# A first weight quarter with a transfer of its own, products by halves of two quarters, and the norm behind them

## The chip, the cores and the metric

One core of one Trainium2 chip. The metric is the device time of one execution in microseconds; the median of three runs stands for a kernel. TensorE is called PE in the rows, VectorE DVE, ScalarE ACT, GpSimd POOL and SyncE SP.

## The reference, cut to what matters

Two transformer blocks run one after the other on 256 tokens of width 1024. Only the first steps of the first block are touched:

```python
h = rmsnorm(x, attn_norm[i])            # x times 1/sqrt(mean(x*x)+eps), times a gain per column
proj = h @ w_in[i]
mq, mk, mv, rq, rk, rv, rg = jnp.split(proj, split_points, axis=-1)
moba_out = ...                          # attention with ALiBi: scores minus slope times distance
ret = ...                               # retention: (q k^T) * decay, times v
ret_out = head_groupnorm(ret, ret_norm[i]) * jax.nn.silu(rg)
```

Everything is float32 in the reference. The kernel forms each float32 product from three products of a high part and a low part.

## The kernel before, in words

**Weights.** All weights lie in HBM as a stream of quarters, 128 partitions x 1024 columns (512 KB) each, in the order of use. SP loads two quarters ("a half" of the stream's blocks) per transfer into `raw`, which has a ring of six quarters; after the first three transfers each next one waits until GpSimd is through with two quarters (semaphore `lo_done`). For each quarter ScalarE writes the rounded high part `w_hi` (`hi`, L635), GpSimd the low part `w_lo = raw - w_hi` in two instructions of 512 columns (`lo`, L594), and TensorE then takes the quarter (`await_quarter`) for 24 products of 256 columns or 12 of 512 columns, three per pair of 128x128 tiles (`three`, L1164). ScalarE keeps four quarters ahead (LEAD), and from the seventh on it waits for `quarter_done` of the quarter six before.

**Blocks of the stream.** Four quarters are a block. The first are RQ (quarters 0 to 3), RK (4 to 7), RV (8 to 11), MQ (12 to 15). A block's result goes to a pair of PSUM banks; pairs 0 and 1 are used in turn, so RV, the third, waits until VectorE has stored RQ out of the first pair (`await_pair`, semaphore `pair_free0`), and MQ until RK is stored (`pair_free1`).

**Order at the start.** Each engine's order is written out by hand. SP: the two halves of x, then three weight transfers. ScalarE: the squares of the second half of x (L657) and their root (L662), the high parts `h_hi` of the turned x (`norm_hi`, L670) with the first two `hi` between them, `hi` of quarters 2 and 3, then `load_constants` (L617 to L620), which issues eight transfers from ScalarE's queue, then `hi` of quarter 4. VectorE: the squares of the first half of x (L2116), the reciprocal root (L2107 to L2110), `widen_root` (L2134), the low parts `h_lo` (`norm_lo`, L2147), the row of roots (L2140); then it waits for all constants, makes the eight ALiBi tables `bias` (L2220), and only then stores RQ and RK (`store_scaled`, L2155) and splits two small inputs (L2227, L2228, L2231). TensorE: 11 filler products on ones (`keep_warm`, L1360), the transposes of x (L1262), 4 fillers, the root spread over a bank (`spread_root`, L1272), 6 fillers, RQ, RK, RV; then MQ with the retention beside it: `ret_scores` (L1343) in front of MQ's first quarter, `ret_out` (L1353) behind it. `ret_out` waits for VectorE's `ret_decay` (L2203) and for the store of RV (L2162), both of which stand behind the tables on VectorE.

```python
act_e.wait_ge(sem("x_loaded"), 16 * NT)
second_squares()
act_e.wait_ge(sem("first_constants"), 32)
norm_hi(0, "attn_norm", (0, 1))
hi(0)
norm_hi(0, "attn_norm", range(2, 6))
hi(1)
norm_hi(0, "attn_norm", (6, 7))
for q in range(2, LEAD):
    hi(q)
load_constants()
```

## Time and profile before

| what | us |
|---|---|
| median of 3 runs (lowest, highest) | 842.63 (842.61, 843.84) |
| the profiled execution's own time | 846.45 |
| its span | 844.6 |
| PE busy in the span | 823.0 |
| POOL busy in the span | 476.0 |

The profile is of one execution; its instructions are told by when they start (us from the span's start) and how long they last. "[2.36 <-DVE work L2155]" behind one is how long its engine sat idle before it and what ended that. The products are pipelined, so their starts are told one after another and their shown lengths overlap.

### The profile page before, as it was taken

To read this page: it belongs to the slowest core of one execution; us is meant where nothing else is said; L and a number is where in the kernel's file an instruction comes from. 1 tells how busy PE (TensorE), PEld (TensorE's weight loads), DVE (VectorE), ACT (ScalarE), POOL (GpSimd) and SP (SyncE) were. 2 spreads that over 40 slices of the span, in tenths; PEclk is the share of its full clock that TensorE was granted. 3 is DMA by queue.
4 is the path that set the end of the run, shared out by engine and by line. 5 is a ranking of instruction groups with operands and counts; after the bars stand their busy time and mean duration, and the time that the engine had idled before them with its cause. 6 is when DMAs were issued, how large, how long until landed. Compare 5 with 4: busy or idle time off the path is not lost.

```text
span 844.6 us, 16277 instructions
## 1 busy us (share of the span) xinstructions
PE 823.0 (97%) x6271; PEld 737.5 (87%) x6271; DVE 496.5 (59%) x1000; ACT 466.3 (55%) x735; POOL 476.0 (56%) x372
## 2 busy tenths in 40 slices
PE   9899999999999999899999999999999999999995
PEld 7899889999999997689988999999889888888883
DVE  3832444682422315663497835347478699999983
ACT  5423654735644466764448433235456578878763
POOL 5997476989999898686854443366868000000000
PEclk9999999999999999999999999999999999999998
DMA  8654144545655554444642213232545689999931
GB/s 315 226 200 177 74 150 175 175 176 199 204 193 199 199 199 150 150 151 150 218 151 100 101 52 102 101 103 100 197 150 177 273 335 370 352 392 340 393 108 50
DMA packets 24141, 160.98 MB, mean 191 GB/s; under 512 B 3200, under 2 KB 3728, under 8 KB 5392
## 3 DMA queue, kind: packets, MB, share of 16 engines
q1 hardware_dynamic: 21456, 154.67, 50.1%
q10 hardware_dynamic: 2624, 5.44, 1.9%
q8 instruction: 44, 0.72, 0.3%
q14 instruction: 17, 0.14, 0.0%
HBM read 157.62 MB, written 1.05 MB: 188 GB/s over the span
## 4 chain that ended last, share of the span: by engine, by line
PE 86%; DVE 7%; ACT 3%; DMA 2%; issue 1%; ACTq 0%; SPq 0%; DVEq 0%
PE bank L1164 72%; PE bank L1713 3%; PE bank L1930 1%; DVE work L2220 1%; DMA row<-dt_bias_dram 1%; PE bank L2047 1%; DMA raw<-weights_dram 1%; DVE work L2529 1%; ACT w_hi L635 1%; PE bank L1262 1%; DVE bank L2589 1%; PE bank L1325 1%; PE bank L1311 1%; DVE best L2588 0%; PE bank L1742 0%
## 5 line engine op out<-in xcount | busy, mean ns | idle before, releaser
L594 POOL TENSOR_TENSOR w_lo<-raw,w_hi 128x512 fp32r<-128x512 f32 x368 | 475.8, 1328 | 175.2 <-ACT w_hi L635 175.1
L1164 PE MATMUL bank<-h_hi,w_hi 128*128 128x256 f32 x864 | 247.4, 286 | 0.5 <-POOL w_lo L594 0.5
L1164 PE MATMUL bank<-h_lo,w_hi 128*128 128x256 f32 x864 | 241.6, 280 | 0.0
L1164 PE MATMUL bank<-h_hi,w_lo 128*128 128x256 f32 x864 | 241.5, 280 | 0.0
L635 ACT ACTIVATE w_hi<-raw 128x1024 fp32r<-128x1024 f32 x184 | 187.9, 1058 | 82.4 <-PE bank L1164 51.2
L1164 PEld LDWEIGHTS bank<-h_hi,w_hi 128*128 128x128 f32 x864 | 162.6, 188 | 4.9 <-POOL w_lo L594 1.4
L1164 PEld LDWEIGHTS bank<-h_hi,w_lo 128*128 128x128 f32 x864 | 163.9, 190 | 0.0
L1164 PEld LDWEIGHTS bank<-h_lo,w_hi 128*128 128x128 f32 x864 | 162.7, 188 | 0.3
L1164 PE MATMUL bank<-w_hi,g_hi 128*128 128x512 f32 x208 | 81.6, 392 | 0.0
L1164 PE MATMUL bank<-w_hi,g_lo 128*128 128x512 f32 x208 | 81.0, 390 | 0.0
L1164 PE MATMUL bank<-w_lo,g_hi 128*128 128x512 f32 x208 | 81.0, 389 | 0.0
L3007 DVE TENSOR_TENSOR w_lo<-raw,w_hi 128x1024 fp32r<-128x1024 f32 x54 | 63.0, 1218 | 5.8 <-ACT w_hi L644 5.6
L1164 PE MATMUL bank<-w_hi,slot_hi 128*128 128x512 f32 x144 | 57.7, 401 | 0.0
L644 ACT ACTIVATE w_hi<-raw 128x1024 fp32r<-128x1024 f32 x54 | 53.6, 1058 | 7.0 <-PE bank L1164 7.0
L1164 PE MATMUL bank<-w_hi,h_hi 128*128 128x512 f32 x128 | 52.6, 411 | 4.0 <-DVE work L2155 2.4
L1164 PE MATMUL bank<-w_hi,slot_lo 128*128 128x512 f32 x144 | 56.3, 391 | 0.0
L1164 PE MATMUL bank<-w_lo,slot_hi 128*128 128x512 f32 x144 | 56.2, 390 | 0.0
L1164 PE MATMUL bank<-w_hi,h_lo 128*128 128x512 f32 x128 | 51.5, 402 | 0.0
L1164 PE MATMUL bank<-w_lo,h_hi 128*128 128x512 f32 x128 | 51.3, 401 | 0.0
L2334 DVE TENSOR_TENSOR bank<-bank,work 128x512 f32<-128x512 f32 x11 | 7.7, 697 | 67.4 <-PE bank L1164 67.4
L1164 PEld LDWEIGHTS bank<-w_hi,g_lo 128*128 128x128 f32 x208 | 39.0, 188 | 8.2
L1164 PEld LDWEIGHTS bank<-w_hi,g_hi 128*128 128x128 f32 x208 | 39.1, 188 | 8.1 <-issue 0.4
(408 smaller groups left out, 1353.9 us busy)
## 6 DMA issues: line engine op xcount, KB each, us to landing
raw<-weights_dram SPq DMA_DIRECT2D x119, 1024.0 KB, 4.8
spare<-weights_dram SPq DMA_DIRECT2D x18, 1024.0 KB, 6.1
tok<-weights_dram SPq DMA_DIRECT2D x9, 1024.0 KB, 5.7
x_sb<-x_dram SPq DMA_DIRECT2D x2, 512.0 KB, 4.6
work<-final_norm_dram ACTq DMA_DIRECT2D x2, 512.0 KB, 5.4
work<-work ACTq DMA_DIRECT2D x8, 128.0 KB, 4.8
work<-constants_dram ACTq DMA_DIRECT2D x1, 640.0 KB, 5.1
con<-constants_dram ACTq DMA_DIRECT2D x1, 520.0 KB, 3.8
```

The lines of the kernel that those rows point to most:

```text
L594: ins = nc.gpsimd.tensor_tensor(w_lo[:, part], raw[:, part], w_hi[:, part].bitcast(F32), ALU.subtract)
L635: nc.scalar.activation(w_hi[:, ring(q)], raw[:, ring(q)], ACT.Copy).then_inc(sem("hi_done"), 1)
L644: nc.scalar.activation(w_hi[:, ring(n)], slot_quarter(i), ACT.Copy).then_inc(sem("slot_hi_done"), 1)
L1164: ins = mm(dst, a, b, start=start and n == 0, stop=stop and n == 2, skip_group_check=True)
L1262: ins = nc.tensor.transpose(bank[turned_bank(n, k)][:, k % 2 * S + t * P:k % 2 * S + (t + 1) * P], x3[:, t, k * P:(k + 1) * P], ident)
L1311: ins = mm(bank[4 + odd][:, t * P:t * P + (t + 1) * P], q3[own, f, t * P:(t + 1) * P], k3[own, kf(f), 0:(t + 1) * P], start=True, stop=True)
L1325: ins = nc.tensor.transpose(bank[6 + n % 2][:, i * P:(i + 1) * P], p[:, i * P:(i + 1) * P], ident)
L1713: ins = mm(bank[b][rows, column + m * w:column + (m + 1) * w], lhs[rows, m, :], rhs[rows, m, :], start=True, stop=True)
L1930: ins = mm(dst, x[t][:, k * P:(k + 1) * P], one_hot[:, t, of], start=t == 0 and x is tok_hi, stop=t == 1 and x is tok_lo, skip_group_check ...
L2047: ins = mm(total[t, c][:, :], one_hot_t[:, tile, t * P:(t + 1) * P], y[:, tile, c * 512:(c + 1) * 512], start=tile == 0 and y is y_hi, sto ...
L2220: V.tensor_scalar(bias[:, h, :], dist, -(HD ** 0.5) * 2.0 ** (-8.0 * (h + 1) / HEADS), None, ALU.mult).then_inc(sem("bias_ready"), 1)
L3007: V.tensor_tensor(w_lo[:, ring(n)], slot_quarter(i), w_hi[:, ring(n)].bitcast(F32), ALU.subtract)\
```

## The change

SP loads quarters 0 and 1 as two transfers, the first with a semaphore of its own. ScalarE makes the high parts of quarters 0 and 1 in halves of 512 columns, between the pairs of `norm_hi`, and does the squares of x and their root only behind `hi(3)`, right ahead of `load_constants`. GpSimd makes the low parts in the order first half of 0, first half of 1, second half of 0, second half of 1. TensorE takes the first halves of quarters 0 and 1, then their second halves, and quarters 2 and 3 by halves too; it spreads the root in front of quarter 3 (into bank 4), and four fillers are gone. VectorE makes `h_lo` first, then the norm, stores RQ before it waits for the constants, then does the splits, stores RK, and makes the tables last. The other edits (`other_sums` in place of `bn_aggr`, and counts raised by seven) change only names and numbers of semaphores.

```diff
@@ -545,7 +545,10 @@
                 sp.dma_start(raw[:, 2 * slot * QUARTER:(2 * slot + 2) * QUARTER], src)\
                     .then_inc(sem(f"half_loaded{slot}"), 16)
 
-            for half in range(3):
+            for part, name in enumerate(("first_loaded", "half_loaded0")):
+                own = slice(part * QUARTER, (part + 1) * QUARTER)
+                sp.dma_start(raw[:, own], weights[0, :, own]).then_inc(sem(name), 16)
+            for half in range(1, 3):
                 load_half(half, half)
             with sp.Fori(0, N_HALVES // 3 - 1) as i:
                 for slot in range(3):
@@ -586,17 +589,21 @@
 
         @block.gpsimd
         def _(pool):
+            def lo_half(r, i):
+
+                part = slice(r % RING * QUARTER + i * (QUARTER // 2), r % RING * QUARTER + (i + 1) * (QUARTER // 2))
+                return nc.gpsimd.tensor_tensor(w_lo[:, part], raw[:, part], w_hi[:, part].bitcast(F32), ALU.subtract)
+
             def lo(n, r):
 
-                pool.wait_ge(sem("hi_done"), n + 1)
-                for i in range(2):
-                    part = slice(r % RING * QUARTER + i * (QUARTER // 2), r % RING * QUARTER + (i + 1) * (QUARTER // 2))
-                    ins = nc.gpsimd.tensor_tensor(w_lo[:, part], raw[:, part], w_hi[:, part].bitcast(F32), ALU.subtract)
-                    if isinstance(n, int) and n == 0 and i == 0:
-                        ins.then_inc(sem("first_low_half"), 1)
-                ins.then_inc(sem("lo_done"), 1)
-
-            for r in range(RING):
+                pool.wait_ge(sem("hi_done"), n + 3)
+                lo_half(r, 0)
+                lo_half(r, 1).then_inc(sem("lo_done"), 1)
+
+            for r, i in ((0, 0), (1, 0), (0, 1), (1, 1), (2, 0), (2, 1), (3, 0), (3, 1)):
+                pool.wait_ge(sem("hi_done"), 2 * r + i + 1 if r < 2 else r + 3)
+                lo_half(r, i).then_inc(sem("lo_done" if i else "first_low_half"), 1)
+            for r in range(4, RING):
                 lo(r, r)
             with pool.Fori(1, N_QUARTERS // RING) as i:
                 for r in range(RING):
@@ -634,6 +641,12 @@
                     act_e.wait_ge(sem("quarter_done"), n - (RING - 1))
                 nc.scalar.activation(w_hi[:, ring(q)], raw[:, ring(q)], ACT.Copy).then_inc(sem("hi_done"), 1)
 
+            def hi_half(q, i):
+
+                act_e.wait_ge(sem("half_loaded0" if q else "first_loaded"), 16)
+                part = slice(q * QUARTER + i * (QUARTER // 2), q * QUARTER + (i + 1) * (QUARTER // 2))
+                nc.scalar.activation(w_hi[:, part], raw[:, part], ACT.Copy).then_inc(sem("hi_done"), 1)
+
             def slot_hi_quarter(i):
 
                 if i >= len(SLOT_ORDER) or SLOT_ORDER[i][1] == WHOLE:
@@ -705,22 +718,25 @@
                     .then_inc(sem("mix_hi_done"), 1)
 
             prepare_root()
-            act_e.wait_ge(sem("x_loaded"), 16 * NT)
-            second_squares()
             act_e.wait_ge(sem("first_constants"), 32)
             norm_hi(0, "attn_norm", (0, 1))
-            hi(0)
-            norm_hi(0, "attn_norm", range(2, 6))
-            hi(1)
+            hi_half(0, 0)
+            hi_half(0, 1)
+            norm_hi(0, "attn_norm", (2, 3))
+            hi_half(1, 0)
+            norm_hi(0, "attn_norm", (4, 5))
+            hi_half(1, 1)
             norm_hi(0, "attn_norm", (6, 7))
             for q in range(2, LEAD):
                 hi(q)
+            act_e.wait_ge(sem("x_loaded"), 16 * NT)
+            second_squares()
             load_constants()
             for q in range(4 * B_WOUT):
                 tick = q - 4 * B_MQ
                 slot = tick - FIRST_TICK
                 if tick == 4:
-                    act_e.wait_ge(sem("other_sums"), 1)
+                    act_e.wait_ge(sem("other_sums"), 8)
                     nc.scalar.activation(stat[:, 128:136], agg[:, :, 1], ACT.Sqrt, bias=eps[:, 1:2])\
                         .then_inc(sem("other_roots"), 1)
                 for n in (2 * slot, 2 * slot + 1):
@@ -1000,7 +1016,7 @@
                 if tick == 4 * (B_PROJ - B_IQ) + 2:
 
                     prepare_root()
-                    act_e.wait_ge(sem("other_sums"), 2)
+                    act_e.wait_ge(sem("other_sums"), 9)
                     nc.scalar.activation(stat[:, 96:112], bank[6][:, 0:16], ACT.Sqrt).then_inc(sem("other_roots"), 1)
                 if tick == 4 * (B_PROJ - B_IQ) + 3:
                     for k in range(4):
@@ -1183,13 +1199,14 @@
             def feature_quarter(n, q, dst, h=(h_hi, h_lo), norm=None, middle=None):
 
 
-                if isinstance(n, int) and n == 0:
-                    pe.wait_ge(sem("first_low_half"), 1)
+                by_halves = isinstance(n, int) and n in (2, 3)
+                if by_halves:
+                    pe.wait_ge(sem("first_low_half"), n + 1)
                 else:
                     await_quarter(n)
                 w = [x.rearrange("p (k c) -> p k c", c=P) for x in quarter(q)]
                 for k in range(KD):
-                    if isinstance(n, int) and n == 0 and k == KD // 2:
+                    if by_halves and k == KD // 2:
                         await_quarter(n)
                     if middle and k == KD // 2:
                         middle()
@@ -1365,10 +1382,25 @@
             pe.wait_ge(sem("x_loaded"), 16 * NT)
             turn_half(0, 0)
             turn_half(0, 1)
-            keep_warm(3, 4, warm)
-            spread_root(0, 2)
             keep_warm(3, 6, warm)
-            feature_project(B_RQ, 0, norm=0)
+
+            def first_quarters_by_halves():
+
+                for half in range(2):
+                    for f in range(2):
+                        if half:
+                            await_quarter(f)
+                        else:
+                            pe.wait_ge(sem("first_low_half"), f + 1)
+                        ins = half_quarter(f, f, bank[0][:, f * S:(f + 1) * S], range(4 * half, 4 * half + 4), 0, f == 0)
+                        if half:
+                            ins.then_inc(sem("quarter_done"), 1)
+
+            first_quarters_by_halves()
+            for f in range(2):
+                if f:
+                    spread_root(0, 4)
+                feature_quarter(2 + f, 2 + f, bank[1][:, f * S:(f + 1) * S])
             pe.wait_ge(sem("root_row_ready"), 1)
             feature_project(B_RK, 1)
             token_project(B_RV, 2)
@@ -2207,20 +2239,15 @@
             V.memset(warm.bitcast(F32), 1.0).then_inc(sem("warm_ready"), 1)
             V.memset(eps[:, 0:1], RMS_EPS)
             V.memset(eps[:, 1:2], GN_EPS).then_inc(sem("constants_made"), 1)
-            dve.wait_ge(sem("x_loaded"), 16 * NT)
-            norm()
-            widen_root()
-            V.tensor_scalar(stat[:, 24:26], stat[:, 4:6], 0.5, None, ALU.mult).then_inc(sem("roots_halved"), 1)
             dve.wait_ge(sem("first_constants"), 32)
             norm_lo(0, "attn_norm")
-            store_root_row(0, 2)
+            dve.wait_ge(sem("x_loaded"), 16 * NT)
+            norm(scratch=bank[5][:, 0:2])
+            widen_root()
+            store_root_row(0, 4)
+            V.tensor_scalar(stat[:, 24:26], stat[:, 4:6], 0.5, None, ALU.mult).then_inc(sem("roots_halved"), 1)
+            store_scaled(B_RQ, 0, rq)
             dve.wait_ge(sem("constants_loaded"), 16 * N_CONSTANT_LOADS)
-
-            for h in range(HEADS):
-                V.tensor_scalar(bias[:, h, :], dist, -(HD ** 0.5) * 2.0 ** (-8.0 * (h + 1) / HEADS), None,
-                                ALU.mult).then_inc(sem("bias_ready"), 1)
-            store_scaled(B_RQ, 0, rq)
-            store_scaled(B_RK, 1, rk)
 
             for hi_, lo_, src in ((p_hi, p_lo, p_raw.rearrange("p (k s) -> p k s", s=S)),
                                   (sm_hi[:, :], sm_lo[:, :], small_raw[:, :])):
@@ -2230,6 +2257,11 @@
 
             V.tensor_scalar(gate_bias[:, :], v("b_gate", 0, 2 * KD), 0.5, None, ALU.mult).then_inc(sem("constants_made"), 1)
             V.memset(root_bias[:, 1:2], 4 * RMS_EPS).then_inc(sem("constants_made"), 1)
+            store_scaled(B_RK, 1, rk)
+            for h in range(HEADS):
+                V.tensor_scalar(bias[:, h, :], dist, -(HD ** 0.5) * 2.0 ** (-8.0 * (h + 1) / HEADS), None,
+                                ALU.mult).then_inc(sem("bias_ready"), 1)
+
             def mix_lo(k, n, gain=None):
 
                 dve.wait_ge(sem("mix_hi_done"), n // 2 * 2 + 2)
@@ -2264,10 +2296,8 @@
                     for g in range(8):
                         dve.wait_ge(sem("bn_stats"), g + 1)
                         ins = V.bn_aggr(agg[:, g, :], bn[:, g, :])
-                        if g < 7:
-                            ins.then_inc(sem("bn_aggr"), 1)
-                    ins.then_inc(sem("other_sums"), 1)
-                    dve.wait_ge(sem("other_sums"), 1)
+                        ins.then_inc(sem("other_sums"), 1)
+                    dve.wait_ge(sem("other_sums"), 8)
                     link(V.tensor_scalar(bank[4][:, 0:8], agg[:, :, 1], GN_EPS, None, ALU.add))
                 if tick == 4:
                     store_scaled(B_MQ, 3, mq)
@@ -2826,7 +2856,7 @@
             for t in range(NT):
                 ins = V.scalar_tensor_tensor(tok3[:, t, 0:512], tok3[:, t, 0:512], 0.5, az[:, t, :], ALU.mult, ALU.mult)
             link(ins)
-            dve.wait_ge(sem("other_sums"), 2)
+            dve.wait_ge(sem("other_sums"), 9)
             dve.wait_ge(sem("other_roots"), 2)
             rsqrt_in(stat[:, 80:96], stat[:, 96:112], o_sums, o_roots)
             for t in range(NT):
```

On ScalarE, from the high parts of quarters 2 and 3 to those of quarters 4 and 5 (`half_loaded` 1 and 2), before:

```order
L635 ACTIVATE w_hi<-raw 128x1024 [waits half_loaded1] x2
L617 DMA con<-constants_dram 128x1040
L617 DMA work<-constants_dram 128x1280
L617 DMA work<-smalls_dram 128x352
L617 DMA work<-p_dram 128x512
L618 DMA work<-positions_dram 128x256
L620 DMA row<-router_b_dram 128x20
L620 DMA row<-a_log_dram 128x8
L620 DMA row<-dt_bias_dram 128x8
L635 ACTIVATE w_hi<-raw 128x1024 [waits half_loaded2] x2
```

and in the changed kernel:

```order
L642 ACTIVATE w_hi<-raw 128x1024 [waits half_loaded1] x2
L670 ACTIVATE tok,stat<-x_sb 128x1024 [waits x_loaded]
L675 ACTIVATE stat<-stat,eps 128x2 [waits first_squares,second_squares]
L624 DMA con<-constants_dram 128x1040
L624 DMA work<-constants_dram 128x1280
L624 DMA work<-smalls_dram 128x352
L624 DMA work<-p_dram 128x512
L625 DMA work<-positions_dram 128x256
L627 DMA row<-router_b_dram 128x20
L627 DMA row<-a_log_dram 128x8
L627 DMA row<-dt_bias_dram 128x8
L642 ACTIVATE w_hi<-raw 128x1024 [waits half_loaded2] x2
```

The squares and root (L657, L662 before; L670, L675 now) and their waits have moved behind the high parts of quarters 2 and 3, and stand directly in front of the eight transfers that lie ahead of quarter 4's high part.

On VectorE, from the row of roots to the first use of the retention scores (`bank` 4 and 5), before:

```order
L2140 COPY work<-bank 128x256 [waits root_spread]
L2220 TENSOR_SCALAR work<-work 128x256 [waits constants_loaded,root_row_ready]
L2220 TENSOR_SCALAR work<-work 128x256 x7
L2155 TENSOR_TENSOR work<-bank,work 128x512 [waits quarter_done] x4
L2227 CAST p_hi<-work 128x512
L2228 TENSOR_TENSOR p_lo<-work,p_hi 128x512 [waits vector_link]
L2227 CAST sm_hi<-work 128x352
L2228 TENSOR_TENSOR sm_lo<-work,sm_hi 128x352 [waits vector_link]
L2231 TENSOR_SCALAR gate_bias<-vec 128x16
L2232 MEMSET root_bias 128x1
L2203 TENSOR_TENSOR work<-bank,work 128x256 [waits ret_scores,bias_ready]
```

and in the changed kernel, where L2187 is `store_scaled`, L2254 to L2258 are the splits and L2262 the tables:

```order
L2172 COPY work<-bank 128x256 [waits root_spread]
L2248 TENSOR_SCALAR stat<-stat 128x2 [waits root_row_ready]
L2187 TENSOR_TENSOR work<-bank,work 128x512 [waits quarter_done] x2
L2254 CAST p_hi<-work 128x512 [waits constants_loaded]
L2255 TENSOR_TENSOR p_lo<-work,p_hi 128x512 [waits vector_link]
L2254 CAST sm_hi<-work 128x352
L2255 TENSOR_TENSOR sm_lo<-work,sm_hi 128x352 [waits vector_link]
L2258 TENSOR_SCALAR gate_bias<-vec 128x16
L2259 MEMSET root_bias 128x1
L2187 TENSOR_TENSOR work<-bank,work 128x512 [waits quarter_done] x2
L2262 TENSOR_SCALAR work<-work 128x256 x8
L2235 TENSOR_TENSOR work<-bank,work 128x256 [waits ret_scores,bias_ready]
```

The store of RQ has come out in front of the wait for the constants; the tables have moved from the front of both stores to behind them.

## Rows read from the trace of the kernel before

**Rows 1.** The page, section 1: busy us (share of the span) and instructions of each engine.

```profile
PE 823.0 (97%) x6271; PEld 737.5 (87%) x6271; DVE 496.5 (59%) x1000; ACT 466.3 (55%) x735; POOL 476.0 (56%) x372
```

**Rows 2.** Waits of PE over the whole span: us in total, times, longest us.

```profile
PE bank L1164 <- DVE work L2155: 2.4, 1, 2.4
```

**Rows 3.** PE's timeline at the start: start us, us, engine, line, op, out<-in, count, [idle before].

```profile
6.55 2.12 PE L1262 MATMUL bank<-con,x_sb 128*128 128x128 f32 x16
8.43 1.18 PE L1360 MATMUL bank<-g_lo 128*128 128x512 f32 x4
...
11.39 0.39 PE L1164 MATMUL bank<-h_hi,w_hi 128*128 128x256 f32 x1
...
15.15 0.38 PE L1164 MATMUL bank<-h_hi,w_hi 128*128 128x256 f32 x1 [0.47 <-POOL w_lo L594]
...
36.83 0.51 PE L1164 MATMUL bank<-w_hi,h_hi 128*128 128x512 f32 x1 [2.36 <-DVE work L2155]
...
41.29 0.39 PE L1164 MATMUL bank<-w_hi,h_hi 128*128 128x512 f32 x1
...
49.53 0.59 PE L1343 MATMUL bank<-work 128*128 128x256 f32 x2
...
53.67 0.38 PE L1353 MATMUL bank<-work 128*128 128x128 f32 x2
```

**Rows 4.** Windows: busy of each engine, granted PE clock, DMA share, GB/s.

```profile
39.00:40.00 1.00, 1.00 (x4) 0.81 (x3) 1.00 (x2) 0.00 (x0) 1.00 (x2) 0.50 0.67 279
354.00:356.00 2.00, 0.00 (x0) 0.00 (x0) 1.58 (x6) 1.75 (x4) 0.00 (x0) 1.00 0.28 119
...
360.00:362.00 2.00, 2.00 (x6) 1.52 (x6) 1.96 (x6) 1.71 (x4) 2.00 (x2) 0.52 0.00 0
436.00:438.00 2.00, 0.80 (x8) 0.52 (x8) 1.97 (x8) 0.00 (x0) 0.95 (x1) 1.00 0.75 311
```

**Rows 5.** VectorE's timeline, same columns as rows 3.

```profile
6.35 1.23 DVE L2116 CUSTOM_DVE_ANT_0 tok<-x_sb 128x1024 f32<-128x1024 f32 x1 [4.93 <-DMA x_sb<-x_dram]
...
25.23 10.35 DVE L2220 TENSOR_SCALAR work<-work 128x256 f32<-128x256 f32 x8 [10.89 <-DMA row<-dt_bias_dram]
35.50 2.47 DVE L2155 TENSOR_TENSOR work<-bank,work 128x512 f32<-128x512 f32 x4
...
42.79 1.26 DVE L2231 TENSOR_SCALAR gate_bias<-vec 128x16 f32<-128x16 f32 x1
...
50.45 0.42 DVE L2203 TENSOR_TENSOR work<-bank,work 128x256 f32<-128x256 f32 x1 [6.40 <-PE bank L1344]
...
51.58 1.40 DVE L2162 TENSOR_SCALAR work<-bank,stat 128x512 f32<-128x512 f32 x2
```

**Rows 6.** ScalarE's timeline and its queue of issues (ACTq), same columns.

```profile
6.35 1.06 ACT L657 ACTIVATE tok<-x_sb 128x1024 f32<-128x1024 f32 x1 [3.17 <-DMA x_sb<-x_dram]
7.32 0.19 ACT L657 ACTIVATION_READ_ACCUMULATOR tok<-x_sb 128x1 f32 x1
...
8.91 1.06 ACT L635 ACTIVATE w_hi<-raw 128x1024 fp32r<-128x1024 f32 x1 [0.20 <-DMA raw<-weights_dram]
9.87 1.55 ACT L670 ACTIVATE h_hi<-bank,vec 128x256 fp32r<-128x256 f32 x4
...
11.40 0.34 ACTq L617 DMA_DIRECT2D con<-constants_dram  x1
...
15.79 0.55 ACTq L620 DMA_DIRECT2D row<-dt_bias_dram  x1
16.39 2.01 ACT L635 ACTIVATE w_hi<-raw 128x1024 fp32r<-128x1024 f32 x2 [1.40 <-issue]
```

**Rows 7.** GpSimd's timeline, first 50 us, same columns.

```profile
10.05 40.24 POOL L594 TENSOR_TENSOR w_lo<-raw,w_hi 128x512 fp32r<-128x512 f32 x31 [9.60 <-ACT w_hi L635]
```

**Rows 8.** Timelines of VectorE and GpSimd around 631 us, same columns.

```profile
631.29 1.23 DVE L2905 TENSOR_TENSOR tok_lo<-tok,g_hi 128x1024 fp32r<-128x1024 f32 x1
...
631.67 2.00 POOL L594 TENSOR_TENSOR w_lo<-raw,w_hi 128x512 fp32r<-128x512 f32 x1 [3.81 <-ACT w_hi L635]
```

## The prediction

> **What bounds the kernel now.** I read the page first: TensorE is busy 97% of the span [rows 1], so a change pays only where TensorE waits, or runs at its lower clock. The list of waits of TensorE over the whole run [rows 2] is headed by 2.4 us for VectorE's store at L2155. TensorE's own timeline [rows 3] places it: RV's first product starts at 36.83 us after 2.36 us of idling, so RK ended at 34.47. RV's first 12 products of 512 columns take from 36.83 to 41.29, 4.46 us; the other 36 run to 49.53, 0.229 us each, or 2.75 for 12. The granted clock [rows 4] says why: in 39 to 40 us it is 0.50 of full, its lower level of 1.2 GHz. That is 1.7 us more, so the wait costs 2.4 + 1.7 = 4.1 us.
>
> VectorE's timeline [rows 5] says why: it sat until 25.23 us for the last constants (dt_bias), made eight tables in 10.35 us (1.3 us each for 256 columns, the length of one GpSimd instruction), and only then, at 35.50, stored RQ, which had been done since about 23.4.
>
> The other limit at the start is the path of the weights. GpSimd works without a gap from 10.05 us, 31 instructions in 40.24 us, 1.30 each and 2.6 us a quarter [rows 7]. TensorE takes 2.76 us a quarter (seven from 15.15 to 34.47 [rows 3]), so it lags GpSimd only slightly: GpSimd was through with quarter 4 at 10.05 + 5 x 2.6 = 23.05, and TensorE began it at 15.15 + 3 x 2.76 = 23.4. Whoever holds up GpSimd by more than 0.35 us there holds up TensorE.
>
> A measurement of this kernel can tell a change of about 0.2%, 1.7 us, from none.
>
> **The change, part by part.**
>
> *Stores ahead of the tables.* The store of RQ now waits only for quarter 3. RV's wait of 2.36 us goes, and the low clock that followed it there. Worth up to 4.1 us.
>
> *First quarter alone.* x landed at 6.35 us and the first 1 MB of weights at 8.91 [rows 5, 6], 2.56 us later; half of it should land at 6.35 + 1.28 = 7.6. One more issue on SP costs about what x's pair did; the queue is full by then, so I cost it at nothing. ScalarE no longer has the squares ahead of `norm_hi`. The transposes run from 6.55 us, 16 in 2.12 [rows 3], so the first four are there at 7.1. Then by the row of four `h_hi` in 1.55 us [rows 6]: two in 0.8 us, to 7.9; quarter 0 in two halves at 0.53 (half of 1.06) to 9.0; two `h_hi` to 9.7; first half of quarter 1 to 10.3. GpSimd starts at 8.5 in place of 10.05, is through with the first half of 0 at 9.8, of 1 at 11.6, then 12.9 and 14.2. TensorE's first product moves from 11.39 to 9.8, when its six fillers (8.43 + 6 x 0.25) end; the four dropped fillers were cover and cost nothing.
>
> *The squares and the constants behind `hi(3)`: the new wait.* In order on ScalarE: 8 x 0.39 + 4 x 0.53 + 2 x 1.0 = 7.2 us from 7.1, so `hi(3)` ends at 14.3. The squares take 1.06 + 0.19 us, to 15.55. The root must wait for them, and all eight issues stand behind that wait. Before, they went out from 11.40 to 16.34 (15.79 + 0.55), 4.94 us, while ScalarE was still at its high parts, and quarter 4 began at 16.39 [rows 6]. Now they go out from 15.6 to 20.5, and quarter 4's high part ends at 21.6, 4.2 us later than before. GpSimd (eight instructions from 8.5, with a gap of 0.5 before the second) is idle by 19.4, or 20.6 with the lock below, and makes quarter 4's low part from 21.6 to 24.2. So RK begins at 24.2, 0.8 us later than the 23.4 of before, though the first product is 1.6 us earlier: quarters 0 to 3 need only 11.0 us of TensorE plus 0.6 for the root's spread.
>
> *The norm on VectorE while GpSimd works.* `h_lo` ends near 13.2. The squares (1.23 us, both inputs in SBUF) and the root's two copies now fall among GpSimd's instructions; before, they ran ahead of them. At 631 us a VectorE instruction with two SBUF inputs ran 1.23 us and the GpSimd instruction started inside it took 2.00 us [rows 8], not 1.3 [rows 7]. I take the same here: VectorE waits for GpSimd's end at 14.2, then holds it 1.2 us. Quarter 2's first half is ready at 16.7 and TensorE waits 0.9 us for it at 15.8; about 1.7 us are left in front of RK, from 22.5 to 24.2. The 24.2 stays, since GpSimd is idle before quarter 4 either way; only the shape of TensorE's wait changes.
> The Trainium skill, page "SBUF — State Buffer", section "Who interferes with whom", says that the pair of ports is locked for a whole instruction and the other side blocks, also for a VectorE instruction with two SBUF inputs. The row agrees for a subtraction; for the squares instruction (L2116) this trace has no case beside GpSimd. Without that lock the whole 2.6 us would stand in one piece before RK, at the same 24.2.
>
> *RK, RV and the clock.* RK takes 11.0 us: 35.2. After the pause before RK the clock may fall again. It did after the pause at 34.47 (2.36 us), and after the one around 355 us (TensorE empty in 354 to 356, clock 0.52 in 360 to 362); it did not around 436 to 438, where 1.2 us of 2 were empty and the clock stayed at 1.00 [rows 4]. My 1.7 us lies between, with 0.9 us of idling shortly before; I take it to fall once, for the same 1.7 us, so RK is done at 36.9. RV follows with no wait (RQ stored by 24, GpSimd through with quarter 8 at 24.2 + 4 x 2.6 = 34.6), 48 products at 0.229 = 11.0, to 47.9. Before: 49.53. **Gain 1.6 us.**
>
> *The cover behind RV.* VectorE now splits first (before from 35.50 + 2.47 to 42.79 + 1.26, 6.1 us [rows 5]), then stores RK (1.2), then makes tables (10.35), then `ret_decay` and the store of RV (2.55: 50.45 to 52.98). The last constant was issued at 15.79 and landed at 25.2, 9.4 us; now issued at 20.0, landing at 29.4. Splits end at 35.5, before RK's 36.9; tables end at 36.9 + 1.2 + 10.35 = 48.5; `ret_decay` and the store would end at 51.0, or 51.7 since the last scores are there at 49.2. TensorE comes to `ret_out` at 47.9 + 4.1 = 52.0 (before, the scores and MQ's first quarter took it from 49.53 to 53.67 [rows 3]). So the tables are hidden by 0.3 to 1.0 us only; a rival rests on this thin cover.
>
> Everything later follows TensorE, so 1.6 us reaches the end. The renamed semaphores cost nothing: same instructions, and the aggregates are waited for once as before.
>
> **The sum.** Against the profiled execution: 846.45 - 1.6 = 844.85 (its span is 844.6, with 1.85 around it). The median of the runs stands 3.8 us below the profiled one; 842.63 - 1.6 = **841.0 us**.
>
> Bounds of the unknowns. Issue of the eight: 4.94 us as before while the DMA engines were full; the first of them took 0.34, so a microsecond less is possible; then GpSimd's 20.6 + 2.6 = 23.2 binds. Clock: nothing or 1.7 us. So without the low clock 842.63 - 3.3 = 839.3, and with quicker issues too 838.3.
>
> **The rivals.**
> 1. *The clock holds.* All as above, but no low stretch in RK: 839.3. For: the pause at 436 us did not lower it. Against: two pauses of over 2 us did. Chance 0.36; with quicker issues besides, 838.3, 0.04.
> 2. *The short transfer doesn't pay: no change.* If each quarter took as long as a half takes now, 2.56 us, quarter 0 would land at 8.9 and quarter 1 at 11.5. ScalarE would wait 1.0 us before the one and 0.8 before the other, RK would start at 26.0, the clock would fall, and the end come at 842.8. Against it: x's two transfers have the same size as these, and the 1 MB queued behind them followed at its full rate. Chance 0.08. The Trainium skill, page "DMA: Bandwidth & Descriptors", section "Bandwidth", has this rule: batch transfers to 1 MiB or more, since each carries a fixed cost. Rows 5 and 6 show the rate of a queued transfer only, and no row here a lone 512 KB one.
> 3. *The tables end too late: slower.* The mechanism: constants land late, so splits, RK's store, tables and the store of RV come late, and TensorE waits at `ret_out`. It decides from a landing of about 31 us on: 31 + 6.1 + 1.2 + 10.35 + 2.55 = 51.2 against TensorE's 50.3 to 52.0. It costs a loss from some 34 on; at 36 us `ret_out` comes at 56.2, 2.5 us later than before: 845.1, more if the clock falls again. For: the issues are 4.2 us later, and quarter loads run beside them. Against: by 8.91 + 2 x 2.56 = 14.0 us the first three transfers are through, which before shared the DMA engines with the constants from 11.40 on. Chance 0.08.
>
> **How the numbers follow.** The forecast, 841.0, has 0.44, give or take 0.9 us. A little under half of it lies past 1.7 us. Faster: 0.21 + 0.35 + 0.04 = 0.60. Within 0.2%: 0.23, 0.01 of rival 1, 0.06 of rival 2 and 0.02 of rival 3 = 0.32. Slower: 0.02 + 0.06 = 0.08. The range goes from rival 1 with quick issues, 838.2, to 843.3 above rival 2; what is left out is most of rival 3 and the edges.
>
> **What would show it.** First product near 9.8 us; the eight issues from about 15.6; quarter 4's high part at 20.5; TensorE idle 1 to 2 us before RK at 24.2; no wait before RV; 12 products of RV per quarter at 0.229; RV's end at 47.9, or 46.2 with the clock at 1.0 throughout; store of RV ahead of `ret_out`. The prediction is wrong if quarter 4's high part comes before 19 us, if the first quarter lands after 8.5 us, or if TensorE waits for a table.

## The result and the profile after

The changed kernel takes 843.73 us, the kernel before, run beside it on the same chip, 842.41 (medians of 22 runs each). The ratio is 1.0014 with a 95% interval of 1.0008 to 1.0019: slower by 1.2 us, give or take 0.5 (the two medians lie 1.3 apart). The forecast was 841.0, with a range up to 843.3. Single executions of the kernel before near 858 us (one here, two beside the experiments) are in a slower state of the chip and are left out of the ratios.

The profiled execution of the changed kernel tells the opposite story: its own time is 842.87 (span 841.1), 3.6 us less than the 846.45 of the profiled execution of before. Both numbers are right. Neither profiled execution is a typical one: that of before lies 4.0 us above the 842.41, that of the changed kernel 0.86 below its median, as the fourth fastest of its 22. What has to be found is which execution the one of before was.

First the places that the prediction named. The timeline of TensorE of the changed kernel (start us, us, engine, line, op, out<-in, count, [idle before]):

```profile
10.10 0.39 PE L1180 MATMUL bank<-h_hi,w_hi 128*128 128x256 f32 x1 [0.35 <-POOL w_lo L595]
...
16.62 0.38 PE L1180 MATMUL bank<-h_hi,w_hi 128*128 128x256 f32 x1 [0.38 <-POOL w_lo L595]
...
23.85 0.36 PE L1180 MATMUL bank<-h_hi,w_hi 128*128 128x256 f32 x1 [0.96 <-POOL w_lo L595]
...
35.23 0.40 PE L1180 MATMUL bank<-w_hi,h_hi 128*128 128x512 f32 x1
...
46.43 0.59 PE L1360 MATMUL bank<-work 128*128 128x256 f32 x2
...
50.49 0.38 PE L1370 MATMUL bank<-work 128*128 128x128 f32 x2
```

The first four rows are the first products of quarter 0, of quarter 2, of RK and of RV; then come the scores and `ret_out` (now L1370). Against [rows 3] the first product is at 10.10 in place of 11.39, RK at 23.85 after a wait of 0.96, RV at 35.23 with no wait, `ret_out` at 50.49 in place of 53.67. ScalarE's timeline and queue, against [rows 6]:

```profile
8.04 1.16 ACT L648 ACTIVATE w_hi<-raw 128x512 fp32r<-128x512 f32 x2
...
14.18 1.08 ACT L670 ACTIVATE tok<-x_sb 128x1024 f32<-128x1024 f32 x1
...
15.53 0.34 ACTq L624 DMA_DIRECT2D con<-constants_dram  x1
...
19.45 0.53 ACTq L627 DMA_DIRECT2D row<-dt_bias_dram  x1
20.03 3.90 ACT L642 ACTIVATE w_hi<-raw 128x1024 fp32r<-128x1024 f32 x4 [4.22 <-issue]
```

The eight issues stand behind the squares and the root, from 15.53 to 19.98, and quarter 4's high part behind them at 20.03. VectorE's timeline, against [rows 5]:

```profile
13.25 2.16 DVE L2148 CUSTOM_DVE_ANT_0 tok<-x_sb 128x1024 f32<-128x1024 f32 x1
...
22.93 1.29 DVE L2187 TENSOR_TENSOR work<-bank,work 128x512 f32<-128x512 f32 x2 [2.20 <-PE bank L1180]
27.88 1.10 DVE L2254 CAST p_hi<-work 128x512 fp32r<-128x512 f32 x1 [3.66 <-DMA row<-dt_bias_dram]
...
36.64 9.88 DVE L2262 TENSOR_SCALAR work<-work 128x256 f32<-128x256 f32 x8
47.35 0.42 DVE L2235 TENSOR_TENSOR work<-bank,work 128x256 f32<-128x256 f32 x1 [0.84 <-PE bank L1361]
...
48.48 1.40 DVE L2194 TENSOR_SCALAR work<-bank,stat 128x512 f32<-128x512 f32 x2
```

RQ is stored at 22.93, ahead of the constants, which landed at 27.88; the tables end at 46.5, 0.84 us before the first scores are there, and the store of RV ends 0.6 us before TensorE asks for it. GpSimd's timeline, against [rows 7], no longer without gaps:

```profile
8.75 1.29 POOL L595 TENSOR_TENSOR w_lo<-raw,w_hi 128x512 fp32r<-128x512 f32 x1 [8.30 <-ACT w_hi L648]
10.52 9.77 POOL L595 TENSOR_TENSOR w_lo<-raw,w_hi 128x512 fp32r<-128x512 f32 x7 [0.48 <-ACT w_hi L648]
21.17 28.99 POOL L595 TENSOR_TENSOR w_lo<-raw,w_hi 128x512 fp32r<-128x512 f32 x22 [0.87 <-ACT w_hi L642]
```

Seven instructions in 9.77 us are 1.40 each where before they took 1.30, and it is idle for 0.87 us before quarter 4. The windows around RK and RV (busy of PE, PEld, DVE, ACT, POOL, then granted clock, DMA share, GB/s), against [rows 4]:

```profile
22.00:24.00 2.00, 1.04 (x9) 0.87 (x8) 1.07 (x2) 1.93 (x3) 2.00 (x3) 1.00 0.62 222
24.00:26.00 2.00, 2.00 (x18) 2.00 (x19) 0.22 (x1) 0.00 (x0) 2.00 (x2) 1.00 0.15 35
...
38.00:40.00 2.00, 2.00 (x10) 1.61 (x9) 2.00 (x3) 1.35 (x2) 2.00 (x3) 1.00 0.79 201
```

The clock stays at 1.00, its upper level of 2.4 GHz, through RK and RV.

### The profile page after: what moved, and what is told of

It reads as the page before. It is cut to its first block, busy times and chain, and to the rows that moved or that the text cites. A ratio compares the mean times of both kernels' runs of the same rounds, so it can differ in the third digit from the quotient of the medians.

```text
span 841.1 us, 16273 instructions
## 1 busy us (share of the span) xinstructions
PE 820.2 (98%) x6267; PEld 734.9 (87%) x6267; DVE 500.5 (60%) x1000; ACT 466.4 (55%) x737; POOL 476.7 (57%) x372
## 4 chain that ended last, share of the span: by engine, by line
PE 87%; DVE 7%; ACT 3%; issue 1%; DMA 1%; ACTq 0%; POOL 0%; SPq 0%; DVEq 0%; POOLq 0%
PE bank L1180 73%; PE bank L1745 3%; PE bank L1962 1%; PE bank L2079 1%; DVE work L2559 1%; DMA raw<-weights_dram 1%; PE bank L1279 1%; DVE bank L2619 1%; PE bank L1342 1%; ACT w_hi L642 1%; PE bank L1328 1%; DVE best L2618 0%; PE bank L1774 0%; PE bank L1833 0%; PE bank L1446 0%
## 5 line engine op out<-in xcount | busy, mean ns | idle before, releaser
L642 ACT ACTIVATE w_hi<-raw 128x1024 fp32r<-128x1024 f32 x182 | 185.4, 1058 | 78.6 <-PE bank L1180 38.0
L657 ACT ACTIVATE w_hi<-raw 128x1024 fp32r<-128x1024 f32 x54 | 53.6, 1057 | 7.0 <-PE bank L1180 7.0
```

Source lines behind the costliest of these rows:

```text
L642: nc.scalar.activation(w_hi[:, ring(q)], raw[:, ring(q)], ACT.Copy).then_inc(sem("hi_done"), 1)
L657: nc.scalar.activation(w_hi[:, ring(n)], slot_quarter(i), ACT.Copy).then_inc(sem("slot_hi_done"), 1)
```

## The experiments

Two theories stood at the start. **A:** the wait of 2.36 us before RV [rows 3] is in the profiled execution of before but in few others, so its removal gives nothing to the median, and the later start of RK stays as a loss. **B:** the wait is in every execution, its removal pays 4.1 us as predicted, and the new front costs 5 us or so that the profile after does not show. A third, **C**, was set up for e5: what the change costs is the squares on VectorE, which hold up GpSimd, and GpSimd's gap ahead of quarter 1's first half. All times are medians; "before" is the kernel before, run beside each. The batches stood on different chips, and the median of before goes from 842.45 (e1 to e4) over 842.52 (e5 to e8) to 843.16 (e9 to e12), so runs of different batches are compared by their ratios to it. A "..." in a code cut marks what is left out.

### e1: the kernel before, once more

No edit.

> The kernel before, unchanged, as a second measurement beside itself. Why: the profiled execution of before took 846.45 us where its 22 runs have a median of 842.41, while the changed kernel's profiled one took 842.87 where its median is 843.73. Theory A (the wait of VectorE's tables before RV, 2.4 us and 1.7 us of low clock, belongs to that one execution and most executions of before do not have it): the new profile shows RV's first product with no wait, or a much shorter one, near 34.5 us, no clock of 0.50 behind it, RV's end near 45.5, and a span near 840.5. Theory B (every execution of before has that wait, and the change gains there and loses elsewhere): the new profile shows the wait of 2.4 us again and a span near 844.6. Both: ratio 1.000 +- 0.001.

Measured: 842.4 (12 runs; before 842.45), ratio 0.9997 (0.9985 to 1.0008). Its profiled execution took 842.26 with a span of 840.5, and looks different. VectorE's timeline of e1:

```profile
24.67 5.07 DVE L2220 TENSOR_SCALAR work<-work 128x256 f32<-128x256 f32 x8 [10.55 <-DMA row<-dt_bias_dram]
29.66 1.27 DVE L2155 TENSOR_TENSOR work<-bank,work 128x512 f32<-128x512 f32 x2
34.30 1.29 DVE L2155 TENSOR_TENSOR work<-bank,work 128x512 f32<-128x512 f32 x2 [3.37 <-PE bank L1164]
```

ScalarE's timeline of e1, at the high parts of quarters 6 and 7:

```profile
24.38 2.01 ACT L635 ACTIVATE w_hi<-raw 128x1024 fp32r<-128x1024 f32 x2 [6.69 <-DMA raw<-weights_dram]
```

GpSimd's timeline of e1, from its gap on:

```profile
25.52 20.21 POOL L594 TENSOR_TENSOR w_lo<-raw,w_hi 128x512 fp32r<-128x512 f32 x15 [0.66 <-ACT w_hi L635]
```

And TensorE's timeline of e1 at RV's first product, with no wait, and at RV's last:

```profile
34.10 0.39 PE L1164 MATMUL bank<-w_hi,h_hi 128*128 128x512 f32 x1
...
44.86 0.39 PE L1164 MATMUL bank<-w_hi,h_lo 128*128 128x512 f32 x1
```

The eight tables took 5.07 us, not the 10.35 of [rows 5]. The row of that group alone gives 279 ns for the shortest, 316 for the median and 1384 for the longest. ScalarE could take up quarter 6 only at 24.38 (23.73 in the profile of before, where GpSimd had no gap), GpSimd ran dry for 0.66 us at 24.9 to 25.5, and VectorE, released by the constants, began the tables at 24.67. The five tables that began by 25.6 took 0.28 to 0.35 us each, the three behind them, beside a busy GpSimd, 1.38. So how long the tables take hangs on whether GpSimd has a gap while they are made, that is, on when two transfers land, quarter 6's weights and the last constants. Of the 95 runs of before that the experiments were compared with, 6 lie above 844.6 (845.0 to 847.8). Theory A holds for e1; RV's last product starts there at 44.86, in the profile of before at 49.31.

The two profiles also differ further on. In e1 the clock falls once more around 434 us, which it did in neither of the two profiles before. The windows of e1:

```profile
434.00:436.00 2.00, 2.00 (x11) 2.00 (x11) 2.00 (x12) 1.02 (x4) 0.00 (x0) 0.50 0.05 12
```

and the same window of the changed kernel:

```profile
434.00:436.00 2.00, 2.00 (x19) 1.67 (x18) 2.00 (x7) 0.00 (x0) 0.00 (x0) 1.00 0.63 266
```

So an end time of one execution holds such differences too, and places near the start are better compared than spans.

### e2: only RQ's store ahead of the constants

```
             store_root_row(0, 2)
+            store_scaled(B_RQ, 0, rq)
             dve.wait_ge(sem("constants_loaded"), 16 * N_CONSTANT_LOADS)
...
-            store_scaled(B_RQ, 0, rq)
```

> Before with one part of the change alone: RQ is stored ahead of the wait for the constants, all else as before. Theory A: nothing to gain in most runs, 842.4 +- 0.6. Theory B: the wait of 2.4 us and 1.7 us of low clock go, 838.3 +- 0.6.

Measured: 842.37, ratio 0.9997 (0.9988 to 1.0006). The part that the prediction paid 4.1 us for is worth nothing in the median. No run of the 11 was above 843.8, so it may cut off the rare late ones; eleven runs are few for that. RV starts at 34.02, as in e1. Its tables took 8.35 us, from 24.62 to 32.97, beside a GpSimd gap of only 0.17 us; with RQ's store (1.3) behind them it would have ended at 34.3, 0.2 us after RV's start. e1 had 3.2 us to spare there (the store done at 30.9). Executions of before lie between much slack and a wait, and the median gains nothing from its removal. Theory B, which needed 838.3, is out.

### e3: the changed kernel with the tables ahead of the stores again

```
-            store_scaled(B_RQ, 0, rq)
             dve.wait_ge(sem("constants_loaded"), 16 * N_CONSTANT_LOADS)
+            for h in range(HEADS):
+                V.tensor_scalar(bias[:, h, :], dist, ...)
+            store_scaled(B_RQ, 0, rq)
+            store_scaled(B_RK, 1, rk)
...
-            store_scaled(B_RK, 1, rk)
-            for h in range(HEADS):
-                V.tensor_scalar(bias[:, h, :], dist, ...)
```

> The changed kernel with VectorE's order of before behind the norm: wait for the constants, tables, RQ, RK, splits. The constants land 2.7 us later than in before (27.8 against 25.2 in the profiles), so the tables end near 38.2 and RV (ready at 35.4) waits some 2.8 us there, with low clock behind it. Theory B: 843.7 + 2.8 + 1.7 = 848.2. Theory A, in which the constants land earlier in unprofiled runs by 3 us or more than the profile of before shows (tables done by 34.5 there): the wait is short, 843.7 to 845.

Measured: 850.06 (6 runs), ratio 1.0079 (1.0062 to 1.0097), above what either theory gave. The tables in VectorE's timeline of e3:

```profile
28.62 9.53 DVE L2251 TENSOR_SCALAR work<-work 128x256 f32<-128x256 f32 x8 [7.93 <-DMA row<-dt_bias_dram]
```

RV's first product in TensorE's timeline of e3:

```profile
39.40 0.80 PE L1180 MATMUL bank<-w_hi,h_hi 128*128 128x512 f32 x1 [3.76 <-DVE work L2187]
```

And the windows behind it (columns as above):

```profile
40.00:42.00 2.00, 2.00 (x6) 1.62 (x5) 1.97 (x3) 0.00 (x0) 2.00 (x3) 0.50 0.46 193
42.00:44.00 2.00, 2.00 (x6) 1.52 (x6) 1.97 (x3) 0.00 (x0) 2.00 (x3) 0.50 0.42 115
```

Here the same order of stores and tables is worth 6.3 us: the change issues the constants 4 us later, so they land at 28.6, the tables get no gap of GpSimd, and RV waits 3.76 us. RV's products then take 13.61 us from the first start to the last (39.40 to 53.01), in the changed kernel 10.97: 2.6 more with the low clock in it, and 3.76 + 2.6 = 6.4 accounts for the 6.3. All six runs lie at 847.3 or above, so the wait is probably in each, though only one was profiled. What theory A added for this run, constants that land 3 us earlier in ordinary runs, is wrong. The change's first part mends what its second part would break.

### e4: quarters 4 and 5 ahead of the squares

```
-            for q in range(2, LEAD):
+            for q in range(2, LEAD + 2):
                 hi(q)
...
-                hi(q + LEAD)
+                if q >= 2:
+                    hi(q + LEAD)
```

> The changed kernel with the high parts of quarters 4 and 5 ahead of the squares and of the eight issues; nothing else. In the changed kernel's profile GpSimd idles 0.87 us before quarter 4 and TensorE 0.96 us before RK. Theory A (the loss of 1.3 us of the changed kernel is this wait behind the issues, with a low clock behind it in some runs): 842.0 to 842.7, at or below before, unless the constants, now issued 2 us later, make the tables late behind RV. Theory B: the wait is worth its 0.96 us at most, 842.8.

Measured: 843.4, ratio 1.0009 (1.0 to 1.0017), 0.3 us below the changed kernel, within the intervals: above both theories. TensorE's wait was not removed but moved to the root's spread (the squares now stand behind two more high parts), and RK began at 23.75, only 0.1 earlier. So e4 does not say what the wait costs. TensorE's timeline of e4:

```profile
20.45 0.71 PE L1290 MATMUL bank<-con,work 128*128 128x128 f32 x4 [0.80 <-DVE work L2167]
```

### e5: the issues ahead of the squares too, the spread in RK

```
             for q in range(2, LEAD):
                 hi(q)
+            load_constants()
+            for q in range(LEAD, LEAD + 2):
+                hi(q)
             act_e.wait_ge(sem("x_loaded"), 16 * NT)
             second_squares()
-            load_constants()
...
-                if f:
-                    spread_root(0, 4)
...
-            feature_project(B_RK, 1)
+            feature_project(B_RK, 1, lambda f: spread_root(0, 4) if f == 2 else None)
```

> The changed kernel with the eight constant loads issued right behind the high part of quarter 3 again, then the high parts of quarters 4 and 5, then the squares and the root; the root is spread in RK in place of ahead of quarter 3. Theory A (the changed kernel lost 1.3 us because quarter 4's high part stood behind the squares and the issues, and gained nothing for it, as most executions of before never wait for the tables): RK starts about 0.7 us earlier than in the changed kernel (23.2 against 23.85), as in before, so 842.4 to 843.0, and no 1 us pause ahead of RK. Rival C (the squares on VectorE, 0.9 us of GpSimd's time, and the gap before quarter 1's first half are what it costs): stays at 843.4 or more.

Measured: 844.47 (before 842.52), ratio 1.0016 (1.0004 to 1.0027): missed, 1.5 us over what theory A gave, and in the range of rival C. RK came at 23.05, as theory A had it. But the root's row now comes at 29.26, RQ's store at 30.43, the tables end at 48.33, and more than was saved in front of RK (a wait of 0.52 in place of 0.96) is lost again at `ret_out`, in TensorE's timeline of e5:

```profile
50.88 0.49 PE L1373 MATMUL bank<-work 128*128 128x128 f32 x2 [0.75 <-DVE work L2194]
```

It is the thin cover behind RV of the prediction, 0.6 us in the changed kernel, spent. But the profiled execution, 843.22, is the fastest of the 12, 1.25 us below the median; what the others lose is not seen in it.

### e6: e5 with both squares on ScalarE

```
+            nc.scalar.activation(tok3[:, 0, :], x3[:, 0, :], ACT.Square, scale=D ** -0.5, accum_out=stat[:, 0:1])...
             second_squares()
...
-            hi_half(0, 1)
+            hi_half(1, 0)
             norm_hi(0, "attn_norm", (2, 3))
-            hi_half(1, 0)
+            hi_half(0, 1)
```

> The kernel of e5, with both squares on ScalarE (VectorE's squares instruction gone) and the high part of quarter 1's first half directly behind that of quarter 0's, so that GpSimd runs from 8.7 us without a gap. GpSimd would be through with quarter 4 at 8.7 + 10 x 1.3 = 21.7, TensorE at best at 9.9 + 11.0 = 20.9 with quarter 3, so RK starts near 22, 1.0 to 1.3 us ahead of before: 841.2 to 841.6. If the tables or a low clock take that back, 842.4.

Measured: 842.68, ratio 0.9998 (0.9986 to 1.0009), 1.3 us over what was expected, though GpSimd ran with one gap of 0.38 us and RK began at 22.84, 1.0 earlier than in the changed kernel. 0.56 us of it is again a wait at `ret_out`, and RQ and half of RK went at TensorE's slower pace, of which more under e9. From e5 to e6 the median falls by 1.8 us, with the squares off VectorE and the halves in another order; the profiles show 0.5 us of that (RV's last product at 45.15 in place of 45.69). Rival C is not ruled out by these two.

### e7: the norm back in front

```
             prepare_root()
+            act_e.wait_ge(sem("x_loaded"), 16 * NT)
+            second_squares()
             act_e.wait_ge(sem("first_constants"), 32)
...
+            dve.wait_ge(sem("x_loaded"), 16 * NT)
+            norm()
+            widen_root()
             dve.wait_ge(sem("first_constants"), 32)
             norm_lo(0, "attn_norm")
-            dve.wait_ge(sem("x_loaded"), 16 * NT)
-            norm(scratch=bank[5][:, 0:2])
-            widen_root()
```

> The changed kernel with the norm (squares, root, its two copies) in front on both engines as before, and so no squares between the high parts and the issues; the split first transfer, the halves and the stores ahead of the tables stay. Theory A: the issues go out at about 12.5 to 17, quarter 4's high part is no longer late, GpSimd starts near 9.3 with its 0.5 us gap: RK starts within 0.3 us of before, 842.4 +- 0.5. Rival C: the same, so this run alone doesn't part them; it says what the halves are worth without the norm's move.

Measured: 842.5, ratio 0.9994 (0.9983 to 1.0005), an interval that lies wholly below the changed kernel's 1.0008 to 1.0019. One part undone gives the whole 1.2 us back: the norm behind the high parts is what makes the change slower. ScalarE's eight issues go out from 12.68, quarter 4's high part comes at 17.67 in place of 20.03, TensorE has no wait before RK, and RK begins at 22.98, RV's last product at 45.25, both 0.9 earlier than in the changed kernel. As the expectation says, this run does not part the late high part from the squares beside GpSimd; both are gone.

### e8: the changed kernel with one transfer of 1 MB

```
-            for part, name in enumerate(("first_loaded", "half_loaded0")):
...
-            for half in range(1, 3):
+            for half in range(3):
...
-                act_e.wait_ge(sem("half_loaded0" if q else "first_loaded"), 16)
+                act_e.wait_ge(sem("half_loaded0"), 16)
```

> The changed kernel with quarters 0 and 1 in one 1 MB transfer again, halves and all else kept. Both theories: the first high part starts at 8.9 in place of 8.04 us and everything behind it on ScalarE moves by that, quarter 4's high part too: 843.7 + 0.8 = 844.5. If ScalarE's chain has slack elsewhere, 843.7.

Measured: 844.26, ratio 1.0018 (1.0006 to 1.003), 0.5 us above the changed kernel, though the two intervals overlap. In its profile the first high part begins at 9.48 in place of 8.04, and all that follows is 1.4 us later, to RV's last product at 47.61. That one pair of profiles flatters the short transfer. Over all profiles of this work the first 512 KB landed between 8.00 and 8.93 us (nine executions, median 8.2), the first 1 MB between 8.61 and 9.45 (five executions, median 8.9): 0.7 us, near the 0.5 of the medians. In each of the nine, quarter 1 landed 1.2 to 1.3 us behind quarter 0, in the changed kernel at 9.30 behind 8.02, half of the 2.5 us between two transfers of 1 MB. So the short transfer does what it says.

### e9, e10, e12: the root's spread issued twice

A detail was still open. Between RK's start and RV's, the changed kernel needs 11.38 us where e1 needs 10.88, at the same clock of 1.00. The timeline of TensorE in RK shows why (the middle one of three products left out). Of e1:

```profile
28.78 0.28 PE L1164 MATMUL bank<-h_lo,w_hi 128*128 128x256 f32 x1
...
29.00 0.28 PE L1164 MATMUL bank<-h_hi,w_hi 128*128 128x256 f32 x1
```

The same view of e7:

```profile
28.86 0.28 PE L1180 MATMUL bank<-h_hi,w_lo 128*128 128x256 f32 x1
...
29.10 0.28 PE L1180 MATMUL bank<-h_lo,w_hi 128*128 128x256 f32 x1
```

Over twelve products the one goes at 0.1133 us each and the other at 0.1178, and it changed at the root's spread, in e5 one way and in e6 the other. The next three runs issue the four products of that spread twice over.

```
-                for t in range(NT):
-                    ins = mm(bank[to][...], ...)
+                for _ in range(2 if n == 0 else 1):
+                    for t in range(NT):
+                        ins = mm(bank[to][...], ...)
```

e9 does this to the changed kernel:

> The changed kernel, with the root's spread in front of quarter 3 issued twice over (the same four products of 128 columns, same values). The question is TensorE's pace: products of 256 columns follow each other at 0.113 us in RK of the kernel before and of e4, and at 0.118 us in RK of the changed kernel, e5 (from the spread on), e7 and e8, all at a granted clock of 1.00; in RV it is 0.229 against 0.233. Theory P: the pace has two values and the four products of a spread turn one into the other (in e5 from the fast to the slow, in e6 from the slow to the fast, at the same place in the code). Then two spreads turn it back: RK at 0.113, RV at 0.229; the added 0.48 us lies in TensorE's wait before RK, and RV's last product comes at 46.20 - 0.43 - 0.21 = 45.6. Rival: the pace follows from what the other engines do beside TensorE, then it stays at 0.118 and 0.233 and RV's last product at 46.2. What the time does depends also on the pace after RV; 843.1 by P if the rest keeps, 843.7 by the rival.

e10 to e6:

> e6 (squares on ScalarE, issues ahead of them, spread in the third quarter of RK) with the spread issued twice. There one spread turned the slow pace into the fast one at 28.5 us. Theory P: with two spreads the pace stays slow, 0.118 us for the last two quarters of RK and 0.233 in RV, where e6 had 0.113 and 0.229; RV's last product at 45.15 + 0.48 + 0.22 + 0.21 = 46.1, the time up by some 0.9 us from e6's 842.7 to 843.6. Rival (pace from the other engines, or from the pause itself): pace as in e6, RV's last product at 45.6, the time up by 0.5 or less.

e12 to e7:

> e7 (everything of the change, but the norm back in front of the high parts) with the spread issued twice. e7 ran RK at the slow pace, 0.118, and RV at 0.233. Theory P: RK at 0.113 and RV at 0.229; RV's last product at 45.25 + 0.48 - 0.55 - 0.21 = 45.0, the time 0.3 us below e7's 842.5. Rival: pace as in e7, RV's last product at 45.7, 0.5 us above e7.

Measured, with before at 843.16 in this batch: e9 843.87 (1.0002, 0.9988 to 1.0015), e10 842.85 (0.9997, 0.9985 to 1.001), e12 843.03 (0.9998, 0.9986 to 1.0011). Theory P falls. e9 went from 0.113 before the spread to 0.118 behind it with eight products, as e7 does with four; e10 from 0.118 to 0.113, as e6. And e12, whose code up to the spread is e7's, came to it at 0.118 and left at 0.113, the other way round from e7, as TensorE's timeline of e12 has it behind the spread:

```profile
28.84 0.28 PE L1180 MATMUL bank<-h_hi,w_hi 128*128 128x256 f32 x1
...
29.07 0.28 PE L1180 MATMUL bank<-h_hi,w_lo 128*128 128x256 f32 x1
```

So the code up to there does not fix the pace: it has two values, and e7 came to the spread at one and e12 at the other. In these traces it changed where the stream of products was broken, though not at every break: in e4 the spread left it at 0.113. The executions profiled are single ones, and the pace of the timed ones isn't seen. In e12's profile RV's last product starts at 44.81, 0.44 earlier than in e7's, though the spread takes 0.44 us longer; the ratios to before, 0.9998 and 0.9994, do not tell the two apart. What sets the pace was not found.

### e11: the kernel before with twelve tables

```
+            for h in range(4):
+                ins = V.tensor_scalar(bias[:, h, :], dist, ...)
+            link(ins)
             for h in range(HEADS):
```

> The kernel before, with four of the eight tables made twice over (12 in all) ahead of the stores, as a dose: how much slack the tables have before RV in ordinary executions. If every execution were like the profiled one of the kernel before (tables 10.35 us, a wait of 2.4 us), four more at 1.3 us would add their full 5.2 us: 847.6 or more. By theory A (in most executions some of the tables run in 0.3 us in a pause of GpSimd, and RQ's store is done at 30.9, 3.2 us before RV at 34.1) only 5.2 - 3.2 = 2.0 us of wait come, plus up to 1.7 us of low clock after it: 844.4 to 846.1, and the profile shows a wait of 1 to 2.5 us before RV. Under 843.2 would mean that the slack is over 5 us.

Measured: 848.72 (10 runs, 845.46 to 854.4), ratio 1.0063 (1.0041 to 1.0086). This is above what theory A gave and in the range that the expectation set for the other case, a wait in every execution. That case cannot stand beside e2, which removed the wait and gained nothing; what e11 shows is that the slack is smaller than the 3.2 us of e1's profile. 848.72 - 843.16 = 5.6 us came of the added 5.2 and the low clock, which cost 1.7 in the profile of before and 2.6 in e3. That leaves 1.3 to 2.2 us of slack in the median. e1's execution was one of the better ones, as the first profile was one of the worse. The profiled execution of e11 was the slowest of its ten: its constants came at 27.86, behind GpSimd's gap (1.00 us, ended at 26.18), none of its twelve tables was a short one, and RV waited 9.66 us, far over the 1 to 2.5 expected, in TensorE's timeline of e11:

```profile
44.24 0.80 PE L1164 MATMUL bank<-w_hi,h_hi 128*128 128x512 f32 x1 [9.66 <-DVE work L2155]
```

## Why the prediction was wrong, by its own steps

*The sum.* This step failed: "The median of the runs stands 3.8 us below the profiled one; 842.63 - 1.6 = 841.0". It took the 3.8 us between the profiled execution and the median for a constant, and subtracted from the median a wait that the median does not have. Those 3.8 us were the wait itself, within 0.3 us of the 4.1 that the text had worked out for it in its first paragraph. e1 and e2 show it: in e1 RV starts at 34.10 with no wait, and e2, which takes the wait away, gains nothing. The gain of 1.6 us was -4.1 for the wait and the clock behind it, +0.8 for the later RK, +1.7 for a clock that falls in RK. Without the first term it is a loss of 2.5, or of 0.8 where the clock holds; the change measured 1.3. The profiled executions differ by -3.6 us, the medians by +1.3, and 4.9 lies between the two. No rival had this, and none of the three signs of being wrong that the prediction named came up in the changed kernel's profile: they asked whether the new order does what was said, not whether the old wait is in every run. The forecast also missed by less than this step alone is worth, by luck: the clock term, wrong by 1.7 us the other way, hid a part.

*The stores ahead of the tables.* Right in that no wait is left before RV, wrong in the price, for the reason above. e3 shows that the changed kernel needs it, at 6.3 us, because its constants land later.

*The first quarter.* First high part at 8.04 (said: 7.9), GpSimd from 8.75 (8.5), first product at 10.10 (9.8). Right. Rival 2 is out: it had quarter 1 land 2.56 us behind quarter 0, and in all nine profiles with the short transfers that was 1.2 to 1.3 us (under e8). The rule of large transfers beside it (the Trainium skill, page "DMA: Bandwidth & Descriptors", section "Bandwidth") does not decide this case; 512 KB behind x's two transfers landed 0.7 us earlier than 1 MB did, by the medians of those profiles.

*The new wait before RK.* Issues from 15.53 (said: 15.6) to 19.98 (20.5), quarter 4's high part at 20.03, RK at 23.85 (24.2). Right within 0.6 us. Against the 23.22 of e1 it costs 0.6, not the 0.8 of the sum. TensorE's wait there was 0.96 us, not 1.7.

*The lock of the ports.* The squares took 2.16 us beside GpSimd against 1.23 before [rows 5]: they waited some 0.9 us, and GpSimd's seven instructions took 0.7 us more than 7 x 1.30. Right in kind, as row and rule (the Trainium skill, page "SBUF — State Buffer", section "Who interferes with whom") had it, and too large in size: the text had GpSimd held 1.2 us and TensorE waiting 0.9 for quarter 2, which measured 0.38. This trace now shows for the squares instruction what the trace of before did not.

*The clock.* It did not fall in RK: rival 1 had this, with 0.36, and RV's last product at 46.20 was its 46.2. A wait of 0.96 us at 22.9, with 0.38 at 16.2, left the clock at 1.00; 2.36 us before RV [rows 3] and 3.76 in e3 did not. Whether it falls there in the timed runs isn't seen, but each has its mean granted clock on record: it is 0.993 or less in 7 of the 22 runs of the changed kernel and in 29 of the 95 of before, the same share, so a low clock does not make the 1.3 us. Rival 3, the only one on the slower side, did not happen either: the constants landed at 27.88. The change is slower by a part of the forecast itself, the later RK, with nothing gained to set against it.

*The cover behind RV.* Tables to 46.5 (said: 48.5, with the fallen clock), 0.6 us of cover at `ret_out` (0.3 to 1.0). Right; e5, e6 and e10 ran into it, with waits of 0.75, 0.56 and 1.52 us.

*What the 1.3 us are.* e7 shows that they come with the norm behind the high parts: with it back in front, the ratio falls from 1.0014 to 0.9994. How they divide is open. In the profiles RV's last product starts at 46.20, in e1 at 44.86: 1.34 later. Of this 0.6 is RK's later start, 0.5 RK's slower pace and 0.2 RV's. The pace varies from one execution to the next, so only the 0.6 is shown to be the change's. The ends of the two executions lie only 0.6 apart (spans 841.1 and 840.5), since e1 lost time to the low clock around 434 us. The late high part of quarter 4 explains the 0.6; whether the squares beside GpSimd (rival C) cost anything besides, no run here shows alone.

## What to carry to other kernels

Before a term of a sum is taken off the median, compare the profiled execution's own time with the runs beside it; where it lies outside them by about the size of the wait that is to be removed, the wait is probably in few others, and a second profile tells, or a run with nothing but that wait removed. A wait that hangs on when two transfers land is such a case. The same holds for small times behind the change: one pair of profiles gave the short transfer 1.4 us, all of them 0.7. Moving work off the front of a kernel pays only if the new place has slack: here each of the places tried (before RK, at the spread, at `ret_out`) had less than 1 us.

## What the runs showed of the hardware beyond this

- VectorE's multiply by a constant on 256 columns (input and output in SBUF) takes 0.28 to 0.35 us in a gap of GpSimd and mostly 1.26 to 1.39 beside its subtractions, so eight of them took 5.07 us in e1, with a gap of 0.66, 8.35 in e2, with 0.17, and 10.35 in the profile of before, with none. TensorE's wait before RV comes out of that.
- TensorE's products of 256 columns follow each other at 0.1133 or at 0.1178 us, those of 512 at 0.229 or 0.233, with the granted clock at 1.00 in both; the difference is 4.5 us per thousand products of either size. It changed at breaks in the stream, and the same code ran at one pace in e7 and at the other in e12. No run here shows what sets it.
